# Hybrid backbone layer on one core: the first modulation in eight chunks of 256 columns instead of four of 512, with its input pieces and the turning of the tokens in smaller steps

## What is computed

```
sh1, sc1, gt1, sh2, sc2, gt2 = adaln(c, w_mod)        # silu(c) @ w_mod + b_mod, 6 x 2048 columns
csh1, csc1, ... = adaln(c_ctx, w_mod)
hx = modulate(rms_norm(x, g_mix), sh1, sc1)           # xn * (1 + scale) + shift
hc = modulate(rms_norm(ctx, g_mix), csh1, csc1)
x_pool, x_u, x_v, x_lru, x_lg, x_q, x_k, x_val = split(hx @ w_in, 8)
c_pool, ..., c_q, c_k, c_val = split(hc @ w_in, 8)
```

## Time and profile before

| | us |
|---|---|
| median of 3 runs | 1684.27 (1683.55 to 1684.93) |
| the profiled execution, its own time | 1683.08 |
| its span, first to last instruction | 1681.4 |
| TensorE busy in the span | 1627.3 |
| VectorE, ScalarE, GpSimd busy | 1095.1, 733.1, 159.2 |

### The profile page before, as it was taken

The page is one execution under the profiler, slowest core; times in us unless marked ns, Lnnn a source line. Parts: engine busy times, 40 slices in busy tenths (PEclk is TensorE's granted clock), DMA queues, the critical chain, the costliest instruction groups (busy, mean ns, idle before and its releaser), DMA issues.

```text
span 1681.4 us, 22407 instructions
## 1 busy us (share of the span) xinstructions
PE 1627.3 (97%) x7679; PEld 1321.5 (79%) x7679; DVE 1095.1 (65%) x1218; ACT 733.1 (44%) x798; POOL 159.2 (9%) x294
## 2 busy tenths in 40 slices
PE   5999999999899999999999899999999999999998
PEld 2468889987678888788878688888888888888876
DVE  2424336787788887788856657767665556456477
ACT  4324224547744434344444643444444444444434
POOL 1002011110002212222100001101100000000000
PEclk9899999999999999999999899999999999999999
DMA  9997457664369979989655468778776566666653
GB/s 354 382 366 226 138 150 226 205 218 148 125 206 330 330 261 327 334 283 332 234 187 186 137 204 277 244 236 288 230 275 194 187 193 189 191 189 188 186 163 138
DMA packets 183862, 389.09 MB, mean 231 GB/s; under 512 B 14368, under 2 KB 14608, under 8 KB 182912
## 3 DMA queue, kind: packets, MB, share of 16 engines
q1 hardware_dynamic: 160784, 312.63, 57.2%
q0 software_dynamic: 23024, 75.74, 12.9%
HBM read 385.30 MB, written 3.01 MB: 231 GB/s over the span
## 4 chain that ended last, share of the span: by engine, by line
PE 88%; DVE 4%; ACT 3%; DMA 3%; issue 1%; SPq 0%; DVEq 0%; ACTq 0%; POOLq 0%
PE ps L1279 24%; PE ps L1281 23%; PE ps L1280 23%; PE ps L1251 4%; PE ps L1252 4%; PE ps L1253 4%; PE ps L1247 2%; PE ps L1332 2%; ACT HI L428 1%; DVE LO L735 1%; DMA BR<-in_w_mod 1%; DMA MR<-in_w_mod 1%; DMA RAW<-in_w_branch 1%; PE ps L1441 0%; PE ps L1455 0%
## 5 line engine op out<-in xcount | busy, mean ns | idle before, releaser
L735 DVE TENSOR_TENSOR LO<-RAW,HI 128x1024 fp32r<-128x1024 f32 x504 | 616.2, 1224 | 449.3 <-ACT HI L428 446.8
L428 ACT ACTIVATE HI<-RAW 128x1024 fp32r<-128x1024 f32 x504 | 533.8, 1061 | 790.7 <-PE ps L1281 680.1
L1279 PE MATMUL ps<-HI,H 128*128 128x512 f32 x1904 | 749.9, 394 | 16.1 <-DVE LO L735 10.9
L1281 PE MATMUL ps<-HI,H 128*128 128x512 f32 x1904 | 743.7, 391 | 0.0
L1280 PE MATMUL ps<-LO,H 128*128 128x512 f32 x1904 | 743.3, 390 | 0.0
L1279 PEld LDWEIGHTS ps<-HI,H 128*128 128x128 f32 x1904 | 359.0, 189 | 96.2 <-DVE LO L735 13.1
L1281 PEld LDWEIGHTS ps<-HI,H 128*128 128x128 f32 x1904 | 358.8, 188 | 75.3
L1280 PEld LDWEIGHTS ps<-LO,H 128*128 128x128 f32 x1904 | 359.3, 189 | 74.6 <-issue 1.2
L392 POOL DMA_DIRECT2D BR<-in_w_mod x208 | 112.1, 539 | 749.5 <-DVE BR L834 329.7
L832 DVE SCALAR_TENSOR_TENSOR BR<-BR,SCF 128x512 f32<-128x512 f32 (+1 forms) x195 | 145.7, 747 | 2.8 <-DMA BR<-in_w_mod 1.4
L1251 PE MATMUL ps<-H,HI 128*128 128x256 f32 (+1 forms) x384 | 126.1, 328 | 0.0
(11 more groups left out here) (252 smaller groups left out, 742.3 us busy)
## 6 DMA issues: line engine op xcount, KB each, us to landing
RAW<-in_w_gate SPq DMA_DIRECT2D x128, 512.0 KB, 4.7
BR<-in_w_mod POOLq DMA_DIRECT2D x208, 256.0 KB, 4.5
RAW<-in_w_ffn_gate SPq DMA_DIRECT2D x88, 512.0 KB, 3.8
RAW<-in_w_ffn_up SPq DMA_DIRECT2D x88, 512.0 KB, 3.8
RAW<-in_w_ffn_down SPq DMA_DIRECT2D x88, 512.0 KB, 3.7
RAW<-in_w_in SPq DMA_DIRECT2D x64, 512.0 KB, 4.5
RAW<-in_w_branch SPq DMA_DIRECT2D x32, 512.0 KB, 4.9
RAW<-in_w_out SPq DMA_DIRECT2D x32, 512.0 KB, 4.0
```

The source lines that it names most:

```text
L428: act.activation(HI[:, j % RING, :], RAW[:, j % RING, :], ACT.Copy).then_inc(hi_done, 1)
L735: tt(LO[:, j % RING, :], RAW[:, j % RING, :], HI[:, j % RING, :], ALU.subtract).then_inc(lo_done, 1)
L1279: mm(o, xh, wh, start=first and t == 0, stop=False, skip_group_check=True)
L1281: i = mm(o, xl, wh, start=False, stop=last and t == 1, skip_group_check=True)
```

## The change

The first modulation is done in eight chunks `c` of 256 columns. A piece of `w_mod` is still 512 KB, now 512 rows x 256 columns, so that a contiguous run in HBM is 1 KB where it was 2 KB. `mod_unit` takes one piece with four matmuls of 256 moving columns; a chunk has eight, and two `mod1_turn` of two matmuls each. One key piece and one query piece belong to a chunk, keys first. The tokens are treated tile by tile: root, reciprocal, scaling and transposes of a tile follow its squares, and the copies of tile k - 1 stand behind the root of tile k on ScalarE and behind the scaling of tile k on VectorE. The first `rows_turn` stands ahead of the modulation. VectorE's and ScalarE's orders follow the chunks.

```diff
-START = []
-for _q in range(4):
-    for _j in range(16):
-        if _j in (9, 13):
-            START.append(("keys", _q, _j // 13))
-        if _q and _j in (3, 7):
-            START.append(("queries", _q - 1, _j // 7))
-        START.append(("mod", _q, _j))
-START += [("queries", 3, 0), ("queries", 3, 1)]
+CHUNKS, CW = 8, 2 * P
+
+
+
+CHUNK_INPUTS = [((2 * c - 1,) if c else (), (2 * c,)) for c in range(CHUNKS)]
+INPUT_AT = [{2: 2 * c - 1, 6: 2 * c} if c else {6: 0} for c in range(CHUNKS)]
+INPUTS = [("queries" if p % 2 else "keys", p // 2) for p in range(2 * CHUNKS)]
+DEAL = ((0,) * 8, (0, 0, 0, 2, 2, 2, 1, 1), *((3, 3, 2, 2, 2, 2, 1, 1),) * 6)
 MOD_RING = 7
-ROWS_TURNED = (0, 0, 4, 10, 16)
...
-            def mod_piece(p, view, q, col):
+            def mod_piece(c, j):
+                p, col = 8 * c + j, (1 - j // 4) * D + c * CW
                 if p >= MOD_RING:
                     sp.wait_ge(s("mod1_used"), p - MOD_RING + 1)
-                sp.dma_start(mod_raw(p).rearrange("p (t n) -> p t n", t=2),
-                             view[:, q, :, col:col + BW]).then_inc(mod1_landed[p % MOD_RING], 16)
-
-            def input_piece(p, q, sl):
+                sp.dma_start(mod_raw(p).rearrange("p (t n) -> p t n", n=CW), v_mod[:, j % 4, :, col:col + CW])\
+                    .then_inc(mod1_landed[p % MOD_RING], 16)
+
+            def input_piece(p):
+                kind, q = INPUTS[p]
+                sl = S_K if kind == "keys" else S_Q
...
-            for kind, q, j in START:
-                if kind == "mod":
-                    mod_piece(16 * q + j, v_mod, j % 8, (1 - j // 8) * D + q * BW)
-                elif kind == "keys":
-                    input_piece(4 * q + j, 2 * q + j, S_K)
-                else:
-                    input_piece(4 * q + 2 + j, 2 * q + j, S_Q)
+            for ch in range(CHUNKS):
+                for j in range(8):
+                    if j in INPUT_AT[ch]:
+                        input_piece(INPUT_AT[ch][j])
+                    mod_piece(ch, j)
+            input_piece(15)
...
+            def rows_columns(k):
+
+                for b in (4 * k, 4 * k + 2):
+                    act.wait_ge(s("x_turned"), b + 1)
+                    act.activation(XT[:, b // 8, b % 4 * 4:b % 4 * 4 + 4, b // 4 % 2 * P:b // 4 % 2 * P + P],
+                                   ps[:, b % 4, :].rearrange("p (k t) -> p k t", k=4), ACT.Copy).then_inc(s("xt_act"), 1)
+
             for k in range(4):
                 act.wait_ge(s(f"tokens{k}"), 16)
                 act.activation(ATT[:, k * D:(k + 1) * D], XTOK[:, k, :], ACT.Square, accum_out=ST[:, k:k + 1])\
                     .then_inc(s("ssq"), 1)
-            act.wait_ge(s("ssq"), 4)
-            act.activation(ST[:, 4:8], ST[:, 0:4], ACT.Sqrt, bias=EPSC[:, 0:1], scale=1.0 / D).then_inc(s("rms"), 1)
-            for b in range(0, 16, 2):
-                act.wait_ge(s("x_turned"), b + 1)
-                act.activation(XT[:, b // 8, b % 4 * 4:b % 4 * 4 + 4, b // 4 % 2 * P:b // 4 % 2 * P + P],
-                               ps[:, b % 4, :].rearrange("p (k t) -> p k t", k=4), ACT.Copy).then_inc(s("xt_act"), 1)
-            for q in range(4):
-                if q:
-                    for t in range(2):
-                        key_high(4 * q - 2 + t)
+                act.wait_ge(s("ssq"), k + 1)
+                act.activation(ST[:, 4 + k:5 + k], ST[:, k:k + 1], ACT.Sqrt, bias=EPSC[:, 0:1], scale=1.0 / D).then_inc(s("rms"), 1)
+                if k:
+                    rows_columns(k - 1)
+            rows_columns(3)
+            for c in range(CHUNKS):
+                for p in CHUNK_INPUTS[c][0]:
+                    key_high(p)
                 for part in range(2):
-                    act.wait_ge(s("mod1_used"), 16 * q + 8 * part + 8)
-                    if q:
-                        act.wait_ge(s("mod1_turned"), 2 * q - 1 + part)
-                    act.activation(MROW[:, part * BW:(part + 1) * BW], ps[:, 6, :], ACT.Copy).then_inc(s("mrow"), 1)
+                    act.wait_ge(s("mod1_used"), 8 * c + 4 * part + 4)
+                    if c:
+                        act.wait_ge(s("mod1_turned"), 2 * c - 1 + part)
+                    act.activation(MROW[:, part * BW:part * BW + CW], ps[:, 6, 0:CW], ACT.Copy).then_inc(s("mrow"), 1)
                     if part == 0:
-                        for t in range(2):
-                            key_high(4 * q + t)
-                for t in range(2):
-                    input_context(2 * q + t)
-                    input_high(2 * q + t)
-            for t in range(2):
-                key_high(14 + t)
+                        for p in CHUNK_INPUTS[c][1]:
+                            key_high(p)
+                input_context(c)
+                input_high(c)
+            key_high(15)
...
-            def rows_turn(b):
-
-                pe.wait_ge(s("rows_scaled"), b // 4 + 1)
-                if b >= 4:
-                    pe.wait_ge(s("xt_dve" if b % 2 else "xt_act"), b // 2 - 1)
-                for k in range(4):
-                    kk = b % 4 * 4 + k
-                    m = turn(ps[:, b % 4, k * P:k * P + P], XTOK[:, b // 4, kk * P:kk * P + P], start=k == 0)
-                m.then_inc(s("x_turned"), 1)
-
-            def mod_pair(q, i):
-
-                part, p = i // 4, 16 * q + 2 * i
-                for p1 in (p, p + 1):
-                    pe.wait_ge(mod1_landed[p1 % MOD_RING], 16 * (p1 // MOD_RING + 1))
-                if i % 4 == 0 and q + part:
-                    pe.wait_ge(s("mrow"), 2 * q + part)
+            def rows_turn(tile):
+
+                pe.wait_ge(s("rows_scaled"), tile + 1)
+                for b in range(4):
+                    if tile:
+                        pe.wait_ge(s("xt_dve" if b % 2 else "xt_act"), 2 * tile - 1 + b // 2)
+                    for k in range(4):
+                        kk = 4 * b + k
+                        m = turn(ps[:, b, k * P:k * P + P], XTOK[:, tile, kk * P:kk * P + P], start=k == 0)
+                    m.then_inc(s("x_turned"), 1)
+
+            def mod_unit(c, i):
+
+                p = 8 * c + i
+                pe.wait_ge(mod1_landed[p % MOD_RING], 16 * (p // MOD_RING + 1))
+                if i % 4 == 0 and p:
+                    pe.wait_ge(s("mrow"), p // 4)
                 for g in range(4):
-                    k = 4 * (i % 4) + g
-                    m = mm(ps[32 * g:32 * g + 32, 6, :], SCP[:, k, :], mod_raw(p + g // 2)[:, g % 2 * BW:(g % 2 + 1) * BW],
+                    m = mm(ps[32 * g:32 * g + 32, 6, 0:CW], SCP[:, 4 * (i % 4) + g, :], mod_raw(p)[:, g * CW:(g + 1) * CW],
                            start=i % 4 == 0, stop=i % 4 == 3, skip_group_check=True, tile_position=(0, 32 * g))
-                m.then_inc(s("mod1_used"), 2)
-
-            def mod1_turn(q, part):
-
-                pe.wait_ge(s("mrow"), 2 * q + part + 1)
+                m.then_inc(s("mod1_used"), 1)
+
+            def mod1_turn(c, part):
...
             pe.wait_ge(s("sc_set"), 1)
-            for i in range(8):
-                mod_pair(0, i)
-                if i < 4:
-                    for b in range(ROWS_TURNED[i], ROWS_TURNED[i + 1]):
-                        rows_turn(b)
-                if i == 5:
-                    params_turn()
-                if i == 6:
-                    mod1_turn(0, 0)
-            mod1_turn(0, 1)
-            for q in range(1, 4):
+            rows_turn(0)
+            for c in range(CHUNKS):
                 for i in range(8):
-                    mod_pair(q, i)
+                    mod_unit(c, i)
+                    if c == 0 and 1 <= i < 4:
+                        rows_turn(i)
+                    if c == 0 and i == 4:
+                        params_turn()
                     if i == 5:
-                        mod1_turn(q, 0)
-                    deal((5 * (q > 1), 5 * (q > 1), 3, 3, 4, 3, 3, 3)[i])
-                mod1_turn(q, 1)
-                deal(3)
+                        mod1_turn(c, 0)
+                    deal(DEAL[c][i])
+                mod1_turn(c, 1)
             for _ in work:
...
```

114 lines of the change are left out of this document (53 added, 61 removed).

## The result

| | before | changed |
|---|---|---|
| median of 20 runs each | 1684.18 us | 1687.22 us |
| lowest to highest | 1682.42 to 1690.44 | 1685.35 to 1689.75 |
| ratio, 95% interval | | 1.0018 [1.0012, 1.0024] |
| profiled execution, span | 1681.4 us | 1684.6 us |
| first key product | 55.41 us | 40.93 us |

The changed kernel is 3.0 us slower: less than the 0.2% named in the prediction, though the interval leaves out no change. It was forecast at 1687.9.

The account below looks back on a forecast made before the run. TensorE was taken as the bound from the first key unit at 41 us; 115.2 us of units, turns, inputs and waits, plus 0.8, put the first value product at 157.0 against 153.44: 1687.9 us, range 1681.0 to 1693.5.

Parts of the forecast that it names:

- What bounds: Before the first value product: the start is bound by arrivals, then TensorE has work without a hole.
- the engines' path: Start: squares, root, scaling, transposes, then chunk 0 turned at 34 to 37 us, plus 3.7 to the first low part.
- A unit at 0.76 us: TensorE: a 256-column modulation unit costs 0.76 us against 1.19 for a pair; bounds 0.60 and 1.19.
- A piece at 1.50 us: DMA: 512 KB of `w_mod` in 1 KB rows takes 1.50 us against 1.36 in 2 KB rows; bounds 1.36 and 1.73.
- the cover: Running chunks: TensorE's 15.4 us a chunk hides the 14.7 us of DMA, unless pieces take over 1.59 us.
- The first key product at 41: The first key unit comes between 39 and 44 us, taken as 41, 14.4 us earlier than before.
- Chunks at 15.4: TensorE needs 15.4 us for a chunk, with no DMA waits behind 50 us.
- The two waits of 0.9: Before the first value product TensorE waits 0.9 us for the last `h_lo` and 0.9 for the copy of key sums.
- The 0.8 us for chunk 1 and the low clock: 0.8 us added for arrivals just late in chunk 1 and some work there at the low clock.
- The rival that held this (0.22): Clock falls in chunks 0 and 1 or tokens come late: first value product at 160 to 162 us; chance 0.22.
- Carried to the end in full: The 3.6 us lost before the first value product lengthen the whole time as much; GpSimd's loads, 6 us later, touch nothing.
- 14.4 us are won by starting early, and 14.5 come back: Early start gains 14.4 us; 31 more units than the 21 pairs behind it cost 14.5, besides turns and waits.

Follow-up runs that it names:

- The tokens alone: The kernel before with root, scaling, transposes and copies of tokens tile by tile, modulation still in groups of 512 columns; median 1684.12 us, ratio 1.0000.
- with 2 KB rows: The changed kernel with each `w_mod` piece read as 256 rows of 2 KB, for its time alone (wrong weights); median 1684.87 us, ratio 1.0004.
- The filled kernel: The changed kernel with 36 unread transposes of the identity added on TensorE where it waited from 34 to 40 us; median 1688.16 us, ratio 1.0024.
- the chunks alone: The changed kernel with the token part as before (one root, transposes behind the second, third and fourth unit of chunk 0); median 1685.04 us, ratio 1.0004.
- In twos: The changed kernel with key and query units dealt behind every second modulation unit only; median 1681.98 us, ratio 0.9985.
- mixed: The changed kernel with two chunks of 256 columns, then three groups of 512 as in the kernel before, token part as before; median 1684.77 us, ratio 0.9997.
- in fours: The kernel with two chunks and three groups of 512, the pairs of those groups taken two by two; median 1682.06 us, ratio 0.9984.
- small chunks at both ends: The kernel of two chunks and three groups, pairs two by two, with its last group also cut into two chunks of 256 columns; median 1683.07 us, ratio 0.9998.

## Why the prediction was right

The forecast, 157.0 us for the first value product and 1687.9 for the run, was right in its mechanism behind the first key product, and nearly in its terms; measured 157.65 and 1687.22. The time of the first key product came out right by luck in part, as told below.

- **What bounds.** Right from the first key product on: TensorE works without a hole but for the two waits at the end. Ahead of it the load of `w_mod` bounds in the changed kernel; the forecast had the engines' path last there (see the first key product, below). The tokens alone show that in groups of 512 columns the tokens don't bind. In chunks they do if they are left as before, by 1.3 us.
- **A unit at 0.76 us.** Measured 0.76, between bounds of 0.60 and 1.19. Two together take 1.20, so 0.32 belongs to the switch, as it was put. One reading under it is shaky: the pair of 1.94 us was taken as one at the lower clock, but the recorded clock of that stretch is 1.00. The number stands all the same, since the pair of 1.93 us at 53.54 lies where the clock was 0.50. The Trainium skill (TensorEngine Tiling (Array Packing), Key Properties) says that a change of the tiling mode drains the TensorE. These rows agree in that a price goes with each switch; that the drain is what it pays for isn't shown.
- **A piece at 1.50 us.** Measured: the twelfth piece landed at 39.87 and the sixteenth at 47.25, with one input piece (1.37) between, so 1.50 each. The estimate from the Trainium skill (DMA: Bandwidth & Descriptors, Why small descriptors are slow) was 1.42, and the measurement decides against it. The statement that the cover hides this after the start is right for the changed kernel (1.1 us at the value product with 2 KB rows), and only just: with the switches fewer it was worth 6.
- **The first key product at 41.** Measured 40.93. The steps: transposes from 13.47 (12.9), last ones done at 29.05 (30), chunk 0 turned at 34.2 (34 to 37), twelfth piece at 39.87 (37.7). The last of these was 2.2 us off. I had taken the whole stream at the 356 GB/s of before with only the 16 narrow rows added. It did not show, since 41 had been taken from the engines' path (37 + 3.7), and that was 3 us too late (`H` was ready at 37.8). So the two paths changed places, their errors offset each other, and the 40.93 is luck: the twelfth piece and its unit at the lower clock, 39.87 + 1.0.
- **Chunks at 15.4.** Measured 15.31, without a wait.
- **The two waits of 0.9.** Measured 0.76 and 0.55, at the places named.
- **The 0.8 us for chunk 1 and the low clock.** Mis-sized: the clock was at its lower level until 46.06, which cost 2.6 us. The filled kernel shows that it is the clock: 2.3 us less from the first key product to the value product. The rival that held this (0.22) was right that the clock would fall and wrong in the price of 160 us and more, since it let the first key product slip to 44. Together: 1.8 more for the clock, 0.5 less for the waits, 0.5 less for six chunks, 0.1 less for the start, 0.7 in all, and 157.65 - 157.0 is 0.65.
- **Carried to the end in full.** Yes, within what two executions differ by: 4.2 us at the value product were 3.2 at the end. GpSimd's loads came 9.4 us later (149.90 against 140.53), not 6, and the end shows nothing of it.

What the prediction did not ask is whether the two parts of the change belong together. It priced the token part by what it makes possible, 12 us earlier transposes, and took no notice that the work it moves away had filled TensorE at the time at which the clock is at stake. By the chunks alone that was worth about 2 of the 3 us lost. And its words "14.4 us are won by starting early, and 14.5 come back" mix two things. By its own prices 6.0 of the 14.5 are five pairs' worth of modulation (5 x 1.19) that stood ahead of the first key product before and simply stand behind it now; only the other 8.6 are the price of small pieces, 26 interruptions more than as many pairs would have made. In twos these 26 were taken away, and 5.1 us came back at the value product.

Open: why the twelfth piece comes 1 us later with the early transposes, and whether the 2 us of the clock can be won back in the median of runs (the filled kernel did not).

## What to carry to other kernels

Cutting work into smaller pieces to start earlier pays the fixed price of each piece for all of it: here 14.5 us earlier against 31 more interruptions. On TensorE the small pieces cost nothing once two of them stood together, as the pair had been (1.20 us against 1.19); what was left then was their price in the transfers, 5.9 us for rows of 1 KB. Price a unit by the same operation at two clock levels, which separates what scales from what doesn't. And at a start with two chains of nearly the same length, here tokens and transfers, making one shorter gains no more than the distance to the other, 1.3 us at most in this case; moving its work can take from TensorE what kept the clock up, which cost 2.3.

## What the runs showed of the hardware

- A modulation unit (eight matmul instructions of 256 columns in four column groups) between full-width matmuls costs 0.76 us, two in a row 1.20, so 0.32 is paid for each interruption, at the high clock.
- In a full queue, 512 KB in 512 rows of 1 KB take 1.50 us, in 256 rows of 2 KB 1.36 to 1.37.
- The granted clock at the start goes with where the transposes stand. It fell to the lower level (1.2 GHz) at 32.4 to 35.9 us in the six kernels in chunks with the early transposes, where TensorE had short units with waits of 0.4 to 2 us between them, and stayed at the higher (2.4 GHz) there in the five in which the last 24 transposes of tokens began at 28 to 29 us. Later it fell in all three mixed kernels: at 55.2 us for 3.4 behind waits of 0.95 and 1.79, and at 79.1 for 3.4 in a wait of 2.7 (mixed); at 51.9 for 6.8 in a wait of 3.1 (in fours); at 53.4 for 3.4 in a wait of 2.95 (small chunks at both ends).
- In the first 20 us and more the recorded clock and the durations don't agree. The clock is given as 1.00, but in the kernel before 16 transposes take 3.68 us at 25.01, and 24 take 2.84 at 29.89. In the changed kernel 16 take 3.65 us at 13.47 and 1.97 at 23.43, and a modulation unit takes 1.08 us at 17.34, as long as where the clock is recorded as 0.50 (38.42), and 0.64 at 22.86. For that stretch the durations are the better guide.
